# Seven-product block multiplication on four more weight tiles of the down projection, with their weight sums made during the head groups

## What is computed

```python
def conv_gated_ffn(h, w_up, conv_w, conv_b, w_down):
    S = h.shape[1]
    u = h @ w_up                                   # (256, 2048) @ (2048, 11264)
    up = jnp.pad(u, ((0, 0), (CONV_W - 1, 0), (0, 0)))
    c = conv_b + sum(up[:, j:j + S] * conv_w[j] for j in range(CONV_W))
    gate, val = c[..., :D_FF], c[..., D_FF:]
    return (jax.nn.silu(gate) * val) @ w_down      # (256, 5632) @ (5632, 2048)
```

## Time and profile before

| what | us |
|---|---|
| median of three executions | 1061.64 |
| the profiled execution, its own time | 1060.14 |
| its span, first to last instruction | 1058.3 |
| TensorE busy in the span | 1048.7 |
| VectorE busy | 787.5 |
| ScalarE busy | 626.9 |
| first matmul of the down projection | at 824.54 |
| first matmul of its second column group | at 937.76 |
| last matmul | at 1050.41 |

### The profile page before, as it was taken

How to read it: one execution, slowest core, us unless ns; L and a number is a source line. 1 busy time by engine, 2 the same in 40 slices (tenths; PEclk the granted TensorE clock), 3 DMA queues, 4 the chain that set the end, 5 groups by cost and what they waited for, 6 DMA issues and landing times.

```text
span 1058.3 us, 17826 instructions
## 1 busy us (share of the span) xinstructions
PE 1048.7 (99%) x5945; PEld 904.9 (86%) x5945; DVE 787.5 (74%) x1174; ACT 626.9 (59%) x971; POOL 86.6 (8%) x150
## 2 busy tenths in 40 slices
PE   9999999999999999999999999999999999999997
PEld 8888888888888888888888888888888888888885
DVE  5677677776555777777777877777877888877777
ACT  6956475756455555555655565555656666646663
POOL 1000000011111010111111010101111000000000
PEclk9999999999999999999999999999999999999999
DMA  9575656587888898998898898989889688887993
GB/s 300 173 231 161 186 169 176 168 256 202 246 252 231 263 250 276 253 270 235 256 275 249 267 237 272 268 256 262 249 259 258 224 294 293 274 298 266 322 316 107
DMA packets 191493, 259.35 MB, mean 245 GB/s; under 512 B 10820, under 2 KB 140580, under 8 KB 191328
## 3 DMA queue, kind: packets, MB, share of 16 engines
q1 hardware_dynamic: 173776, 215.32, 63.1%
q0 software_dynamic: 17360, 43.22, 18.7%
q10 hardware_dynamic: 320, 0.34, 0.1%
HBM read 256.73 MB, written 44.06 MB: 284 GB/s over the span
## 4 chain that ended last, share of the span: by engine, by line
PE 98%; DMA 1%; DVE 0%; SPq 0%; ACT 0%; issue 0%; DVEq 0%
PE tr_ps L1579 15%; PE pj L1579 15%; PE pj L1331 9%; PE pj L1581 8%; PE tr_ps L1581 8%; PE pj L1319 5%; PE pj L1320 5%; PE pj L1321 5%; PE pj L1333 5%; PE sc_ps L1319 4%; PE sc_ps L1321 4%; PE sc_ps L1320 4%; PE pj L1346 3%; PE pj L1348 1%; PE tr_ps L1320 1%; PE tr_ps L1321 1%
## 5 line engine op out<-in xcount | busy, mean ns | idle before, releaser
L889 DVE TENSOR_TENSOR split<-raw,split 128x1024 fp32r<-128x1024 f32 x266 | 321.7, 1223 | 146.7 <-ACT split L578 141.4
L578 ACT ACTIVATE split<-raw 128x1024 fp32r<-128x1024 f32 x260 | 270.7, 1057 | 97.2 <-PE pj L1581 28.7
L1579 PE MATMUL tr_ps<-act_split,split 128*128 128x512 f32 x704 | 245.5, 392 | 0.0
L1579 PE MATMUL pj<-act_split,split 128*128 128x512 f32 x704 | 245.0, 391 | 0.0
L1581 PE MATMUL pj<-act_split,split 128*128 128x256 f32 x704 | 197.6, 281 | 0.0
L1581 PE MATMUL tr_ps<-act_split,split 128*128 128x256 f32 x704 | 197.6, 281 | 0.0
L1168 DVE TENSOR_TENSOR split<-raw,split 128x1024 fp32r<-128x1024 f32 (+1 forms) x124 | 137.2, 1136 | 37.9 <-ACT split L834 35.7
L834 ACT ACTIVATE split<-raw 128x1024 fp32r<-128x1024 f32 (+1 forms) x124 | 119.5, 987 | 69.0 <-PE sc_ps L1321 31.9
L1579 PEld LDWEIGHTS tr_ps<-act_split,split 128*128 128x128 f32 x704 | 131.8, 187 | 28.5
L1579 PEld LDWEIGHTS pj<-act_split,split 128*128 128x128 f32 x704 | 131.7, 187 | 28.6
L1331 PE MATMUL pj<-act_split,split 128*128 128x512 f32 x416 | 147.1, 398 | 0.0
(11 more groups left out here) (240 smaller groups left out, 1512.6 us busy)
## 6 DMA issues: line engine op xcount, KB each, us to landing
raw<-w_up SPq DMA_DIRECT2D x176, 512.0 KB, 6.0
raw<-w_in SPq DMA_DIRECT2D x72, 512.0 KB, 3.8
raw<-w_down SPq DMA_DIRECT2D x68, 512.0 KB, 5.6
t_dram<-w_down POOLq DMA_DIRECT2D x60, 512.0 KB, 6.5
raw<-t_dram SPq DMA_DIRECT2D x40, 512.0 KB, 5.7
raw<-w_o SPq DMA_DIRECT2D x32, 512.0 KB, 5.7
t_dram<-t_dram POOLq DMA_DIRECT2D x40, 256.0 KB, 6.0
raw<-w_down SPq DMA_DIRECT2D x20, 256.0 KB, 5.6
```

Of the source, the lines that this page charges most:

```text
L578: ins = act.activation(hi[:, slot, 0:TILE], raw[:, slot, 0:TILE], ACT.Copy)
L889: dve.tensor_tensor(lo[:, slot, 0:n], raw[:, slot, 0:n], hi[:, slot, 0:n].bitcast(F32), ALU.subtract).then_inc(lo_done, 1)
L1579: pe.matmul(up_banks[v][b], wh[:, c, b * P:(b + 1) * P], act_both(k), start=k == 0, stop=False, skip_group_check=True)
```

## The change

The second column group multiplies fourteen tiles (4 to 17) by seven block products, and the first still ten. Where each stands in the second group is set anew: the sums tiles now begin after the third plain place instead of the fifth, and stand in runs of two and three. The activation sums of the four new tiles (14 to 17) are made during the second group, and go into the places of `s_hi`, `s_lo` that the second group's first four sums tiles have freed. The weight sums now have twelve turns. Two of them are issued during the head groups, step by step between `copy_group_a` of the four groups, for which GpSimd's loop over the groups is written out; the other ten stand where the ten stood. The load of `gfin`, which shares memory with the buffer of the activation sums, waits for the last of them.

```diff
-SUM_KT = tuple(range(4, 14))
-PLAIN_KT = tuple(kt for kt in range(DOWN_TILES) if kt not in SUM_KT)
-SUMS_AFTER = ((5, 6, 7, 10, 11, 12, 15, 16, 19, 20), (4, 5, 7, 8, 9, 10, 12, 13, 14, 15))
+SUM_KT = (tuple(range(4, 14)), tuple(range(4, 18)))
+SUMS_HELD = len(SUM_KT[0])
+PLAIN_KT = [tuple(kt for kt in range(DOWN_TILES) if kt not in SUM_KT[g]) for g in range(2)]
+SUMS_AFTER = ((5, 6, 7, 10, 11, 12, 15, 16, 19, 20), (2, 2, 3, 3, 3, 4, 4, 5, 5, 5, 6, 6, 7, 7))
...
+SUMS_NEW = {t: SUM_KT[1].index(d[3]) for t, d in enumerate(DOWN)
+            if d[1:3] == ("sums", 0) and (d[0] == 0 or d[3] not in SUM_KT[0])}
+SUMS_USED = [t + 4 for t, d in enumerate(DOWN) if d[:3] == (1, "sums", 0)]
...
+EARLY_TURNS = 2
+EARLY_STEPS = {0: ((0, 0), (0, 1)), 1: ((0, 2), (0, 3), (0, 4)), 2: ((1, 0), (1, 1), (1, 2)), 3: ((1, 3), (1, 4))}
...
-    first, last = T_WO - 10, T_DOWN - 2
-    return first + (turn * TURN_DMAS + k) * (last - first) // (TSUM_TURNS * TURN_DMAS)
+    if turn < EARLY_TURNS:
+        first, last, turns = T_QUAD + 8, T_WO - 10, EARLY_TURNS
+    else:
+        first, last, turns, turn = T_WO - 10, T_DOWN - 2, TSUM_TURNS - EARLY_TURNS, turn - EARLY_TURNS
+    return first + (turn * TURN_DMAS + k) * (last - first) // (turns * TURN_DMAS)
...
-            copy_group_a(0)
-            with pool.Fori(1, QUADS) as j:
-                pool.wait_ge(mixlo_s, j * 2)
+            for j in range(QUADS):
+                if j > 0:
+                    pool.wait_ge(mixlo_s, j * 2)
                 copy_group_a(j)
-                pool.tensor_copy(fq[:], fcum[:, :, bass.ds(j * 4, 4)]).then_inc(fq_s, 1)
-
-            for turn in range(TSUM_TURNS):
-                weight_sums(turn)
+                if j > 0:
+                    pool.tensor_copy(fq[:], fcum[:, :, j * 4:j * 4 + 4]).then_inc(fq_s, 1)
+                for turn, step in EARLY_STEPS[j]:
+                    weight_sums(turn, step)
+
+            for turn in range(EARLY_TURNS, TSUM_TURNS):
+                for step in range(5):
+                    weight_sums(turn, step)
 
             pool.wait_ge(z_s, 8)
+            pool.wait_ge(slo_s, len(SUM_KT[1]))
...
                 act.wait_ge(s_fp, 4 * q + 4)
-                act.activation(s_hi[:, q], sums[:, 0:384], ACT.Copy)
+                if q >= SUMS_HELD:
+                    act.wait_ge(mm_done, T_DOWN + SUMS_USED[q - SUMS_HELD])
+                act.activation(s_hi[:, q % SUMS_HELD], sums[:, 0:384], ACT.Copy)
...
             for t in range(DOWN_END):
-                if t > 0 and t + 5 < GROUP_END[0] and DOWN[t + 5][:3] == (0, "sums", 0):
-                    add_values(sums_index(t + 5))
-                if t > 0 and t + 4 < GROUP_END[0] and DOWN[t + 4][:3] == (0, "sums", 0):
-                    sums_lo(sums_index(t + 4))
+                if t > 0 and t + 5 in SUMS_NEW:
+                    add_values(SUMS_NEW[t + 5])
+                if t > 0 and t + 4 in SUMS_NEW:
+                    sums_lo(SUMS_NEW[t + 4])
                 if 0 < t and t + LEAD < DOWN_END:
                     down_lo(t + LEAD)
```

More of the change, by code:

```diff
@@ L68, in down_plan @@
     for g in range(2):
-        for i, (half, kt) in enumerate((half, kt) for half in range(2) for kt in PLAIN_KT):
+        for i, (half, kt) in enumerate((half, kt) for half in range(2) for kt in PLAIN_KT[g]):
             plan.append((g, "plain", half, kt))
-            if i in SUMS_AFTER[g]:
-                plan += [(g, "sums", part, SUM_KT[SUMS_AFTER[g].index(i)]) for part in range(4)]
+            for kt, after in zip(SUM_KT[g], SUMS_AFTER[g]):
+                if after == i:
+                    plan += [(g, "sums", part, kt) for part in range(4)]
     return plan
@@ L838, in sums_hi @@
                 act.wait_ge(s_fp, 4 * q + 4)
-                act.activation(s_hi[:, q], sums[:, 0:384], ACT.Copy)
-                act.activation(g_hi[:, 2 * SUM_KT[q], P:2 * P], sums[:, 384:512], ACT.Copy).then_inc(shi_s, 1)
+                if q >= SUMS_HELD:
+                    act.wait_ge(mm_done, T_DOWN + SUMS_USED[q - SUMS_HELD])
+                act.activation(s_hi[:, q % SUMS_HELD], sums[:, 0:384], ACT.Copy)
+                act.activation(g_hi[:, 2 * SUM_KT[1][q], P:2 * P], sums[:, 384:512], ACT.Copy).then_inc(shi_s, 1)
             for t in range(DOWN_END):
@@ L847, in _ @@
                     down_hi(t + LEAD)
-                if 0 < t < GROUP_END[0] - 5 and DOWN[t + 5][:3] == (0, "sums", 0):
-                    sums_hi(sums_index(t + 5))
+                if 0 < t and t + 5 in SUMS_NEW:
+                    sums_hi(SUMS_NEW[t + 5])
                 for g in range(2):
@@ L1176, in add_values @@
                     dve.wait_ge(s_fp, 4 * q)
+                if q == SUMS_HELD:
+                    dve.wait_ge(comb_s, 8)
                 dve.tensor_tensor(whole[:], g_hi[:, blocks].rearrange("p b n -> p (b n)").bitcast(F32),
@@ L1617, in down_sums @@
                 g, kind, part, kt = DOWN[t]
-                q, slot = sums_index(t - part) % len(SUM_KT), t % RING
+                first, q, slot = kt == SUM_KT[g][0], SUM_KT[g].index(kt) % SUMS_HELD, t % RING
                 def g_part(a):
@@ L1649, in _ @@
                     pe.wait_ge(comb_s, 4)
-                if DOWN[t][1:3] == ("sums", 0) and kt == SUM_KT[0]:
+                if DOWN[t][1:3] == ("sums", 0) and kt == SUM_KT[g][0]:
                     if g == 0:
@@ L1655, in _ @@
                         pe.wait_ge(z_s, 8)
-                if g == 0 and kind == "sums" and part == 1:
-                    pe.wait_ge(slo_s, SUM_KT.index(kt) + 1)
+                if kind == "sums" and part == 1 and t - 1 in SUMS_NEW:
+                    pe.wait_ge(slo_s, SUMS_NEW[t - 1] + 1)
                 pe.wait_ge(lo_done, T_DOWN + t + 1)
```

70 lines of the change are left out of this document (32 added, 38 removed).

## The result

| | before | after |
|---|---|---|
| median, us | 1061.72 | 1072.01 |
| executions | 6 | 6 (1070.65 to 1073.97) |
| ratio to before | | 1.0098, 95% interval 1.0085 to 1.0111 |
| first matmul of the down projection | 824.54 | 829.97 |
| first matmul of the second column group | 937.76 | 944.12 |

The change makes the kernel 10.3 us slower. I had predicted 1064.3 us, 2.7 slower, and at most 1069.0, so the sign was right and the time lies outside the range. The profiled execution of after took 1073.97 us, 2 above its median. For the experiments an excess over the kernel before is worked out as (ratio - 1) x 1061.7 us; with it after is at +10.4. All experiments were compared with the kernel before on the same chip (medians 1061.5 to 1061.9).

A forecast was written before the change was run, and what follows sets the result against it. TensorE, busy 99% of the span, was taken to bound the kernel; -2.7 for matmuls, +3.4 for VectorE and +2.0 for loads gave +2.7 on the median 1061.64, so 1064.3 us, range 1061.0 to 1069.0.

The forecast's parts named there:

- 12 matmuls less: Four second-group tiles of the down projection go from 24 matmuls to 21, taking 2.72 us off TensorE's path.
- VectorE's additions: Activation sums of four new second-group tiles, 2.40 us each, make TensorE wait 3.4 us (bounds 2.4 and 4.4).
- loads of the dense stretch: 28.3 MB from third plain place to end of tile 17 cost 2.0 us, between 0 and 7.3.
- VectorE's budget: VectorE's work against TensorE's from tile 13 part 2 to tile 16 part 3, leaving 3.4 us of waiting.
- ScalarE's waits for `raw`: Sign that loads bind: ScalarE waits for raw in the second group's runs of three; no size given.
- landings over 6 us: Sign that loads bind: landings over 6 us and a DMA share near 1.0 before tile 13.
- 1.2 and 0.8: Parts of the dense stretch's 2.0 us: 1.2 for too low a mean load rate, 0.8 for unevenness.
- What is moved: Two turns of weight sums go into the head groups at no cost, up to 1.5 us if loads come late.
- Rival 4: Sums DMAs in the head groups make loads late behind the attention: about +1.5 us, total 1065.8; chance 0.05.
- the upper end above: Loads of the dense stretch at 316 to 322 GB/s would cost 7.3 us; gfin's megabyte was counted in here.
- The lead at tile 13: VectorE is 2.3 us ahead when it has split part 2 of tile 13; named the likeliest error if larger.

The follow-up runs named there:

- light loads, no additions: Changed down projection without the four new weight sums and activation sums, second-group weight-sum loads halved, against the kernel before: 1059.37 us, ratio 0.9981.
- with and without: Halved second-group weight-sum loads: with the new activation sums and gfin loaded later 1063.11 us, ratio 1.0015; without those sums 1059.37 us, ratio 0.9981.
- full against light loads: Second-group weight-sum loads whole or halved: with additions and gfin later 1065.26 against 1063.11 us; without additions 1061.3 against 1059.37 us.
- `gfin` later: Changed down projection without the four new weight sums, gfin's load put one place behind the last sums tile: 1065.26 us, +4.2 instead of +7.0.
- head alone: Kernel before plus four more tiles' weight sums, unused, two turns in the head groups, old down projection: 1064.25 us, ratio 1.0029, +3.1 us.
- step moved: As head alone, but the second turn's accumulating pair issued behind the fourth group's copy instead of in the third: 1061.62 us, ratio 1.0001.
- the other order that was tried: Full change with the accumulating pair and gfin's load moved later, plus new sums tiles placed between held ones: 1065.68 us, ratio 1.0032; 1066.06 without the new order.
- the kernel with twelve tiles: Second group with tiles 4 to 15, spread out, one turn in the head groups, gfin's load later, against the kernel before: 1061.63 us, ratio 0.9997.
- twelve turns ahead of the down projection: Kernel before with twelve weight-sum turns, all between head groups and down projection: 1063.11 us, ratio 1.0031; six executions 1061.0 to 1063.1, five 1066.7 to 1071.1.

## Why the prediction failed

| step | predicted, us | measured, us | by |
|---|---|---|---|
| 12 matmuls less | -2.7 | -2.0 | light loads, no additions |
| VectorE's additions | +3.4 | +3.6 (3.37 in the trace); +4.6 with full loads | with and without |
| loads of the dense stretch | +2.0 (0 to 7.3) | +1.6 to +2.6 | full against light loads |
| `gfin` | 0 | +2.8 | `gfin` later |
| head groups | 0, up to 1.5 | +3.1 | head alone, step moved |
| sum | +2.7 | +10.4 | |

Each row of the measured column is uncertain by 1 to 2 us. Additions and loads are not independent: 3.6 with 2.6, or 4.6 with 1.6, is 6.2 for both. With that the rows add up to 10.1.

**The two terms that I had worked out came out right.** VectorE's budget gave 3.4 us in pieces at part 3 of tiles 13 to 16 and the places behind, and with light loads there are 3.37 at those places. The loads came to some 2 us as said, ScalarE's waits for `raw` rose as said, and the share was 0.94 to 0.96 up to tile 13; the landings over 6 us that I had named as a sign didn't come. There is luck in this term. I took 339 GB/s as what the engines can do, and called 352 more than every rate shown, but the same trace has 399 over five microseconds, and in the experiments twenty microseconds passed at 368 and others at 332, both with the engines full. And of the 2.0 I had chosen 1.2 and 0.8 more than worked them out.

**"Nothing, then; up to 1.5 us if loads come late once in each of three groups"** is the first step that failed, in "What is moved". I had compared mean rates: 58 GB/s more on 172 at a share of 0.58. The cost came from when and where. GpSimd's issues don't follow the tile counts, since the wait of `copy_group_a` holds them back until 158 us and each then waits for the one before. I looked at that coupling in one direction only: whether the issues make a copy late. And the accumulating pair cost nothing right behind an attention block and 3 us ahead of one, where VectorE's late split stands in front of the attention's reductions. Rows 2 and 14 showed the last group without a wait, beside a pair whose two DMAs were issued 8 us apart, at 232.95 and 241.10 us, and told nothing of a pair 10 us ahead of the scores. Rival 4 had late loads here, but behind the attention, with a chance of 0.05 and half the size. (8.4 MB over 150 us are 56 GB/s and not 58; nothing hangs on it.)

**"Its megabyte goes through the end of the dense stretch, which is in the upper end above"** is the second. I had seen where the load goes, and then gave it no term. One megabyte at the 339 GB/s of the earlier trace rows is, by estimate, 3 us of all DMA engines, at the end of a stretch where, by my own sum, nothing was to spare; 2.8 were measured. The added wait that moves it was in the diff, and cost about as much as the matmuls give.

**The range** took the lower terms at their forecast and the uncertain ones up to the loads' bound; it had no room for two terms of 3 us that stood at zero. The lead at tile 13 (2.3 us), which I had named as the most likely error, was right: with light loads VectorE was done with part 2 at 1000.10, some 2.1 us before TensorE would have begun part 3.

## What to carry over

A term set to zero needs its own check of time and place: for every DMA that a change moves, look what releases its issue and which load is next in line there, not what the mean rate of the stretch is. A lead that a ring of four places limits to 0.65 us is spent once, by a late load or by extra work, so new work on a stretch whose loads keep the DMA engines full costs both, and the other order that was tried didn't help there. A tile that gives 0.68 us and asks for 2.4 us of additions and 1.83 MB in 4.8 us cost more than it gave without plain places beside it, and gave nothing that could be measured with them.

## What the runs showed of the hardware

- **Behind a wait of 2.6 us TensorE's clock was halved.** The last matmul before it started at 189.62 and the next at 192.46; in that time the granted clock fell from 1.00 (2.4 GHz) to 0.50 (1.2 GHz), with 1.5 us lost on top. Behind the wait of 1.44 us in the kernel with the head groups alone the next pairs keep 0.35 us and the granted clock 1.00, so there was no such loss. Waits of 0.2 to 1.9 us in after's down projection are each followed by one matmul of 0.33 to 0.34 us instead of 0.23, some 0.1 more.
- **Accumulating DMAs between places in HBM delay weight loads.** With two of them in flight the loads of the same microseconds took 10.8 us instead of 4.5, and without them in the same place at most 6.1. The window 176 to 182 moved 223 GB/s at a full share of the DMA engines, less than the 347 GB/s at 0.96 of the dense stretch. One such DMA alone, at 119.41 us in the kernel with twelve tiles and 12 us ahead of the scores, brought the loads behind it to 7.8 us at most, and TensorE didn't wait. No run put plain copies of the same size in the pair's place, so how much of this is the accumulating is not shown:

```profile
176.00:182.00 6.00, 6.00 (x46) 5.09 (x48) 3.74 (x4) 2.61 (x3) 0.00 (x0) 1.00 1.08 223
```

- **TensorE has a slower pace at the same granted clock.** In seven of the fourteen profiled executions, of several kernels, a head group takes 52.3 to 52.4 us instead of 51.83 without a wait, in others not; it may be part of the 2 us by which executions of one kernel differ. In the one with twelve turns ahead of the down projection the whole up projection ran so, 1.7% slower, with a matmul of 512 columns listed at 398 instead of 391 ns. That kernel had the highest DMA share there (0.93 to 0.96 against 0.87 to 0.91 before), which may or may not be the cause: six of its executions with the same DMAs took no longer than 1063.11 us.
